# A value stage in groups of eight experts: 256 columns per unit, quarter rows summed in PSUM, remainders in place

## What is computed

```
top-16 of 256 key pairs per head -> idx, gate = softmax(top_s)     # 8 heads, 16384 experts
u = u_tab[idx]; act = gelu(einsum('thkd,td->thk', u, hb))
v = v_tab[idx]
out = einsum('thk,thkd->td', gate * act, v)
```

## Time and profile before

| what | value |
|---|---|
| median of three runs | 3581.84 us |
| profiled execution | 3567.09 us |
| its span | 3565.3 us |
| TensorE matmuls busy | 3327.1 us (93%) |
| VectorE busy | 2497.0 us (70%) |
| GpSimd busy | 2373.4 us (67%) |
| ScalarE busy | 1104.7 us (31%) |

### The profile page before, as it was taken

One profiled execution on the slowest core, in us unless ns is written; L12 is line 12 of the kernel. 1 busy time (PEld: TensorE's weight loads), 2 busy tenths in 40 slices (PEclk: granted clock), 3 DMA queues, 4 the chain that ended last, 5 costly groups with the idle time before them and its releaser, 6 DMA issues. The chain is left out here.

```text
span 3565.3 us, 59397 instructions
## 1 busy us (share of the span) xinstructions
PE 3327.1 (93%) x22639; PEld 3127.5 (88%) x22639; DVE 2497.0 (70%) x4249; ACT 1104.7 (31%) x1497; POOL 2373.4 (67%) x1923
## 2 busy tenths in 40 slices
PE   7999987889998999999999999998999999999997
PEld 7988853547998999999999999998989888989897
DVE  7842223325216999996787666556999999999996
ACT  4111132343223233444444444322222222222223
POOL 2533307003443458888888888887989888989894
PEclk9999989999999999999999999999999999999998
DMA  4598978672322235888888888887888888878883
GB/s 160 191 364 308 357 271 279 226 263 95 140 103 89 82 117 200 318 328 344 338 322 351 331 340 342 339 309 291 328 331 316 312 328 322 325 307 326 317 328 138
DMA packets 251873, 969.63 MB, mean 272 GB/s; under 512 B 44930, under 2 KB 109059, under 8 KB 173187
## 3 DMA queue, kind: packets, MB, share of 16 engines
q1 hardware_dynamic: 151650, 553.25, 42.5%
q0 software_dynamic: 57344, 335.58, 23.2%
q10 hardware_dynamic: 42720, 78.87, 6.0%
HBM read 891.32 MB, written 73.92 MB: 271 GB/s over the span
## 5 line engine op out<-in xcount | busy, mean ns | idle before, releaser
L129 POOL TENSOR_TENSOR wl<-raw,wh 128x512 fp32r<-128x512 f32 x1280 | 1750.8, 1401 | 722.5 <-ACT wh L122 719.0
L122 ACT ACTIVATE wh<-raw 128x1024 fp32r<-128x1024 f32 x648 | 650.6, 1052 | 1871.6 <-PE acc L1558 602.9
L1932 PE MATMUL acc<-vh,wh 128*128 128x360 f32 x2048 | 681.6, 333 | 91.2 <-DVE xt L2021 57.2
L1556 PE MATMUL acc<-hh,wh 128*128 128x360 f32 x2048 | 677.4, 331 | 8.3 <-POOL wl L129 8.3
L1934 PE MATMUL acc<-vh,wl 128*128 128x360 f32 x2048 | 674.4, 329 | 0.0
L1933 PE MATMUL acc<-vl,wh 128*128 128x360 f32 x2048 | 671.2, 328 | 0.0
L1558 PE MATMUL acc<-hh,wl 128*128 128x360 f32 x2048 | 671.1, 328 | 0.0
L1557 PE MATMUL acc<-hl,wh 128*128 128x360 f32 x2048 | 670.8, 328 | 0.0
L147 PE MATMUL acc<-hh,wh 128*128 128x256 f32 (+1 forms) x1920 | 546.8, 285 | 7.6 <-DVE tt L427 5.0
L148 PE MATMUL acc<-hl,wh 128*128 128x256 f32 (+1 forms) x1920 | 544.1, 283 | 0.0
L149 PE MATMUL acc<-hh,wl 128*128 128x256 f32 (+1 forms) x1920 | 542.4, 283 | 0.0
(11 more groups left out here) (360 smaller groups left out, 4466.9 us busy)
## 6 DMA issues: line engine op xcount, KB each, us to landing
raw<-units SPq DMA_DIRECT2D x324, 1024.0 KB, 4.9
kr<-cache_k SPq DMA_DIRECT2D x128, 512.0 KB, 6.6
vr<-cache_v SPq DMA_DIRECT2D x128, 512.0 KB, 5.8
expert_acts<-ast ACTq DMA_DIRECT2D x128, 180.0 KB, 5.1
expert_gates<-gs ACTq DMA_DIRECT2D x15, 1536.0 KB
a<-expert_acts SPq DMA_DIRECT2D x32, 720.0 KB, 9.4
g<-expert_gates SPq DMA_DIRECT2D x16, 1440.0 KB, 7.3
output_steps<-qo ACTq DMA_DIRECT2D x16, 288.0 KB, 7.4
```

The lines of the kernel that those rows point to most:

```text
L122: act.activation(m.wh[s][:, k:k + KT // 2, :], m.raw[s][:, k:k + KT // 2, :], ACT.Copy).then_inc(m.hi_done, 1)
L129: x = pool.tensor_tensor(m.wl[s][:, part, :], m.raw[s][:, part, :], m.wh[s][:, part, :].bitcast(F32), ALU.subtract)
L1556: pe.matmul(o, m.wh[s][:, k, :], m.hh[:, k, N0:T], start=(k == 0), stop=False)
L1932: pe.matmul(o, m.wh[s][:, 4 * e + d, :], vh[gg][:, e, :], start=(e == 0), stop=False)
```

## The change

Groups are eight blocks of experts (`GRP = 8`, 16 groups), a unit holds 256 columns of eight blocks, so a group takes eight units (`UPG = 8`) of two tiles (`VT = 2`) of 24 matmuls. The tiles use two PSUM banks, `acc[:, 0, d]`. The quarter rows' sum `yx` is the bank `acc[:, 1, 0]`, copied to `yx_sb` at the end and turned into `acc[:, 1, 1]`. The remainders `vl` lie over the weighed activations: `vl0` is written where `a40` is, `vl1` where `a41` is. Weighing, rounding and remainders go in halves of four blocks. Activations are loaded for eight blocks at once (1440 KB), gates for one group of eight (1440 KB) behind unit n = 5, and those of the second group ahead of the first load of a unit in the stage. Rows go 9 in 8 units. TensorE waits for the first weighed blocks one by one. Buffers are moved so that all this fits; the value weights lie in the new order in memory.

```
-GRP, NG = 4, 32
+GRP, NG = 8, 16
+UPG, VT = 8, 2
...
-    m.first_acts = at("a40", [P, GRP, ND], off=first); m.gates = at("g8", [P, NB, 2 * GRP, BW], off=first + GRP * ND * 4)
+    m.first_acts = at("a40", [P, GRP, ND], off=first); m.gates = at("g8", [P, NB, GRP, BW], off=first + GRP * ND * 4)
...
 def sums_by(j):
-    return min(HK, max(0, (j - 2) * 14 // 13))
+    return min(HK, max(0, (j - 2) * 9 // 8))
 def rows_by(j):
-    return min(HK, j * 14 // 13)
+    return min(HK, j * 9 // 8)
 def sums_x_by(j):
-    return min(HK, max(0, (j - 3) * 14 // 13))
+    return min(HK, max(0, (j - 3) * 9 // 8))
 def rows_x_by(j):
-    return min(HK, max(0, (j - 1) * 14 // 13))
+    return min(HK, max(0, (j - 1) * 9 // 8))
...
+    vl = [at("vl0", [P, GRP, ND], F32R, off=m.first_off), at("vl1", [P, GRP, ND], F32R, off=m.top - GRP * ND * 4)]
     vh = [at(f"vh{s}", [P, GRP, ND], F32R) for s in range(2)]
-    vl = [at(f"vl{s}", [P, GRP, ND], F32R) for s in range(2)]
...
+    yx = m.acc[:, 1, 0, :]
+    halves = [slice(GRP // 2 * h, GRP // 2 * (h + 1)) for h in range(2)]
...
+                for n in range(UPG):
+                    if end and n >= UPG - 2:
                         continue
+                    load_unit(m, sp, i * (2 * UPG) + (U_EXP_V + UPG * gg + n + 2), n % 2)
+                    if n == 1 and not end:
+                        load_acts(sp, g, 1 - gg)
+                    if n == 5 and not end and not (last and gg == 0):
+                        load_gates(sp, g)
+        def load_acts(sp, g, s):
+            sp.wait_ge(S["tile_done"], g * (UPG * VT) + 1)
+        def load_gates(sp, g):
+            sp.wait_ge(S["weighed"], g * GRP + 2 * GRP)
...
+            sp.wait_ge(S["weighed"], GRP)
+            sp.dma_start(m.gates[:, :, :, :].rearrange("p b e n -> p b (e n)"), m.gD[:, :, GRP:2 * GRP, :].rearrange("b p e n -> p b (e n)")).then_inc(m.gates_in, 16)
...
+            def w_hi(g, s, h):
+                act.wait_ge(S["weighed"], g * GRP + (GRP + GRP // 2 * (h + 1)))
+                act.wait_ge(S["tile_done"], g * (UPG * VT) + 1)
+                act.activation(vh[s][:, halves[h], :], a4[s][:, halves[h], :], ACT.Copy).then_inc(S["weighed_hi"], GRP // 2)
...
+                        if n in (3, 4) and not end:
+                            w_hi(i * 2 + gg, 1 - gg, n - 3)
...
+                        for d in range(VT):
+                            pe.wait_ge(S["sum_added"], i * (2 * UPG * VT) + (UPG * VT * gg + VT * n + d + 1))
+                            o = m.acc[:, 0, d, 0:ND]
                             for e in range(GRP):
+                                if n == 0 and d == 0:
+                                    pe.wait_ge(S["weighed_lo"], i * (2 * GRP) + (GRP * gg + e + 1))
...
+                                mm = pe.transpose(m.acc[:, 1, 1, P * c:P * c + P], yx_sb[:, P * c:P * c + P], m.ident[:, :])
...
+                    for d in range(VT):
+                        r = VT * j + d
                         dve.wait_ge(S["tile_done"], r + 1)
+                        x = m.xt[:, VT * n + d, N0:T]
+                        dve.tensor_tensor(x, x, m.acc[:, 0, d, 0:ND], ALU.add).then_inc(S["sum_added"], 1)
+                        if d == 0:
                             for k in range(sums_by(j), sums_by(j + 1)):
                                 add_row(k)
+                        if d == 1:
                             for k in range(sums_x_by(j), sums_x_by(j + 1)):
                                 add_row_x(k)
+                        if g == NG - 1 and VT * n + d >= 3:
+                            add_square(VT * n + d - 3)
+                        if d == 0 and g + 1 < NG and n in (3, 4):
+                            weigh(g + 1, n - 3)
+                        if d == 1 and g + 1 < NG and n in (4, 5):
+                            low(g + 1, n - 4)
...
-    values = peer_v[0].reshape(NG, GRP, P, 4, 512).transpose(0, 3, 2, 1, 4).reshape(P, P, D)
+    values = peer_v[0].reshape(NG, GRP, P, UPG, VT * P).transpose(0, 3, 2, 1, 4).reshape(P, P, D)
```

More of the change, by code:

```diff
@@ L1820, in turn_loads @@
                 g = i * 2 + gg
-                for n in range(4):
-                    if last and gg == 1 and n >= 2:
+                end = last and gg == 1
+                for n in range(UPG):
+                    if end and n >= UPG - 2:
                         continue
[L1824 to L1828, removed]
-        def load_acts(sp, g, s):
[L1831 to L1836, removed]
+                    load_unit(m, sp, i * (2 * UPG) + (U_EXP_V + UPG * gg + n + 2), n % 2)
[3 more added lines that the diff above has]
+                        load_gates(sp, g)
+        def load_acts(sp, g, s):
+            sp.wait_ge(S["tile_done"], g * (UPG * VT) + 1)
+            sp.dma_start(a4[s][:, :, :], m.aD[ds(g * GRP + GRP, GRP), :, :].rearrange("e p n -> p e n")).then_inc(ain[s], 16)
+        def load_gates(sp, g):
+            sp.wait_ge(S["weighed"], g * GRP + 2 * GRP)
+            sp.dma_start(m.gates[:, :, :, :].rearrange("p b e n -> p b (e n)"), m.gD[:, :, ds(g * GRP + 2 * GRP, GRP), :].rearrange("b p e n -> p b (e n)")).then_inc(m.gates_in, 16)
         def load_tiles(eng, n):
@@ L1893, in turn @@
                 for gg in range(2):
[L1894 to L1900, removed]
+                    end = last and gg == 1
+                    for n in range(UPG):
+                        if not (end and n >= UPG - 2):
+                            split_hi(m, act, i * (2 * UPG) + (U_EXP_V + UPG * gg + n + 2), n % 2, i * UPG + ((U_EXP_V + UPG * gg) // 2 + n // 2 + 1),
+                                     (S["tile_done"], i * (2 * UPG * VT) + (UPG * VT * gg + VT * (n + 1))))
+                        if n in (3, 4) and not end:
+                            w_hi(i * 2 + gg, 1 - gg, n - 3)
+                        if last and gg == 0 and n == UPG - 2:
                             act.wait_ge(S["rows_added"], HK)
                             for g in range(4):
[L1903 to L1906, removed]
+                                act.activation(y_sb[:, 512 * g:512 * g + 512], m.aux[:, g, :], ACT.Copy)
+                            act.wait_ge(S["x_added"], HK)
+                            act.activation(yx_sb[:, :], yx, ACT.Copy).then_inc(S["y_kept"], 1)
+                        if end and n >= 1:
+                            for k in range(VT * n - 2, VT * n):
                                 square(k)
@@ L1910, in _ @@
             turn(NG // 2 - 1, True)
-            for k in range(KT - 4, KT):
+            for k in range(KT - 2, KT):
                 square(k)
@@ L1935, in turn @@
+                                pe.matmul(o, m.wh[s][:, VT * e + d, :], vh[gg][:, e, :], start=(e == 0), stop=False)
+                                pe.matmul(o, m.wh[s][:, VT * e + d, :], vl[gg][:, e, :], start=False, stop=False)
+                                mm = pe.matmul(o, m.wl[s][:, VT * e + d, :], vh[gg][:, e, :], start=False, stop=(e == GRP - 1))
                             mm.then_inc(S["tile_done"], 1)
-                        if last and gg == 0 and n == 3:
+                        if last and gg == 0 and n == UPG - 1:
@@ L2003, in _ @@
-            dve.sem_inc(S["weighed_lo"], 1)
-            for g in range(NG):
-                for n in range(4):
-                    j = 4 * g + n
-                    if g == 0:
-                        dve.wait_ge(x_in[n], 16)
-                    if j == N_EXP - 4:
+                dve.tensor_tensor(a, a, m.gates[:, :, e, :], ALU.mult).then_inc(S["weighed"], 1)
+                if e > 0:
+                    first_low(e - 1)
+            first_low(GRP - 1)
+            for g in range(NG):
+                for n in range(UPG):
+                    j = UPG * g + n
+                    if g == 0 and n % 2 == 0:
+                        dve.wait_ge(x_in[n // 2], 16)
+                    if j == N_EXP - UPG:
@@ L2035, in _ @@
+            for k in range(KT - 3, KT):
+                add_square(k)
             dve.wait_ge(S["root_ready"], 2)
```

101 lines of the change are left out of this document (34 added, 67 removed).

## The result

The changed kernel takes 3614.12 us (median of four runs, 3603.36 to 3615.49), against 3581.11 us before: a ratio of 1.0093, 95% interval 1.0078 to 1.0109. It is 33 us slower where I had forecast 30 us faster. The profiled execution took 3603.4 us, span 3601.5, 36 us more than that of before. The first value matmul starts at 2423.3 us, the last at 3577.5: 1154 us for the stage in place of 1121, and 3.3 us lost ahead of it. (Those lie in the stages before: the first weighing starts at 2421.64 us where it was 2415.81, and the profiled executions of the experiments put the first value matmul anywhere from 2416.8 to 2426.3.)

What follows compares the result with a forecast made beforehand. VectorE was taken as full in the value stage, GpSimd just behind. GpSimd's new pace -41, late rows +11, start +2 and end -2 gave -30 us off the median 3581.8: 3552, range 3540 to 3570.

Steps and rivals of the forecast that it cites:

- What bound the kernel before: Value stage: VectorE full at 8.7 of 8.76 us a unit, its quarter row the odd one, GpSimd just behind.
- Step 2: Quarter row's sum moved to PSUM: 0.68 us instead of 2.61, leaving VectorE 5.8 us a unit.
- Step 3: GpSimd is the next bound in the value stage at 8.50 us a unit: 1080 us against 1121, 41 less.
- Step 4: Two PSUM banks for sums instead of four: late rows delay VectorE's sums, 11 us given back.
- rival C: Late rows and starved remainders meet two banks, holding TensorE, ScalarE and GpSimd: about 3604 us; chance 0.17 with everything above 8.86.
- C's sign: TensorE waiting over 5 us a group for the sum of the second tile.
- Rival D: Quarter row stays slow in PSUM, its delays hit two banks; chance 0.09 together with whatever ends at nothing.
- Step 6: Weights behind the 1440 KB activation load land in 7.2 us, inside 8.7: no cost, at most 60 us.
- The landing by ring order: Weights queued behind the whole activation load by the ring-order rule: 3.7 us late, landing at 8.6, just inside 8.7.
- The sign that I had set for this: ScalarE waiting for weights after the activations, with landings over 9 us.
- Step 7: Stage's start and end: plus 2 us for eight weighings and gates before the first unit, minus 2 at the end.
- The sum: All terms for the whole kernel: -41 + 11 + 2 - 2 = -30 us, giving 3552.

Runs made afterwards that it cites:

- e10b: The kernel before with the quarter rows' additions reading their second operand from PSUM, their sum left out (no kernel to use): 3536.9 us, ratio 0.9882.
- e7: e4 with every gathered row added one unit later: 3530.0 us, ratio 0.9864.
- e4: The changed kernel with TensorE's inner loop of two units, first two units of weights ahead of the gates, and activations in two 720 KB halves: 3536.6 us, ratio 0.9882.
- e8: e4 with the quarter rows' sum back in SBUF as before the change: 3571.6 us, ratio 0.9988.
- e9: e8 with the tiles' sums in four PSUM banks instead of two: 3562.8 us, ratio 0.9952.
- e1: The changed kernel with TensorE's loop as an inner loop of two units instead of sixteen in one body: 3582.5 us, ratio 1.0009.
- e11: The changed kernel with only the activations loaded in two halves of 720 KB: 3577.4 us, ratio 1.0011.
- e6: The changed kernel with TensorE's inner loop of two units and the activations in two 720 KB halves: 3538.1 us, ratio 0.9885.
- e12: e7 with a group's activations in one load of 1440 KB again: 3567.8 us, ratio 0.9979.
- e5: The changed kernel with TensorE's inner loop of two units and the first two units of weights ahead of the gates: 3569.2 us, ratio 0.9979.
- e3: The changed kernel with the first two units of weights sent ahead of the second group's gates: 3605.2 us, ratio 1.0079.

## Why the prediction was wrong

- **What bound the kernel before** was read rightly, as far as e10b shows: one operand of one instruction moved to PSUM brings 42 us, mostly waits of TensorE for VectorE, which the quarter row had made full.
- **Step 2**: 0.68 us forecast for the quarter row, 0.748 measured, 740 to 758 without spread. VectorE is busy 610 of 930 us, 66%, where I said near 70.
- **Step 3**, GpSimd next at 8.50 us a unit, holds once the other causes are gone: 8.4 in e7, with TensorE's waits at GpSimd. In the changed kernel itself GpSimd rested 150 us.
- **Step 4**, 11 us for late rows and two banks, had about the right size: 6 in e4 to e7, which noise could hide, and 13 for the banks with slow quarter rows (e8 to e9). What e1 shows late is partly another thing than the step had: the sum of the next unit, behind a remainder held up to over 6 us, which only rival C named. Still, that 3614 lies near C's 3604 is luck. In the changed kernel TensorE's waits for sums are fewer than before the change, 79 us by both records or 4.9 a group where C's sign was over 5, and the time went elsewhere. Rival D is out by the quarter row's time.
- **Step 6 failed**, "stays inside 8.7", valued at nothing with 60 us as the bound. It costs 29 to 44 us (e11, e6, e12). I added 2.3 us for 720 KB to a quiet unit's landing of 4.9. But rows (two of 1 MB at the start of a group), the unit before and the activations are in flight together, and the weights behind took 13.8 us. The landing by ring order beside the step came to 8.6, also short: it too left the gathers out. The sign that I had set for this, landings over 9 us after the activations, came, and rival C had the activations and two rows sharing the DMA; the step's own sum had not.
- **A term was missing: code.** I counted 6144 matmuls of the same form and did not ask how TensorE gets them. The body of the loop doubled in length, code is fetched through the whole stage, and this costs 30 us (e1). The twelve pauses alone are 28 us, with the low clock behind them on top; a part was spared elsewhere, as the waits of e1 show. Nothing in the trace of before shows it, but the number of instructions in a body can be counted from the change, and no sentence bounded it.
- **Step 7**, plus 2 for the start: 11 us (e5; e3's 5 agree within noise), and the trace shows both parts. ScalarE took the first unit 25.1 us after the first weighing, 13.9 before the change and 15.2 by the forecast. The eight weighings were given 0.465 us each, but they alternate with remainders, 0.9 an expert as the same step says, so the gates went out 6.6 us behind the first weighing and not 3.7. And I took one landing beside gates, 10.9, for a moment at which four loads of `xt`, 1040 KB each, were in flight or had just landed as well; it was 17.7. At the end, where minus 2 was forecast, 24.1 us behind the last matmul became 24.0.
- **The sum**, re-sized: e4, the change without the three, is 42 us faster than before, where I had forecast 30, with 11 given back at step 4 that measured 6 to 13. On it lie 35 for the activations (e4 to e5), 11 for the start (e5 to e1) and 30 for code (e1 to the change), which make 34 slower, against 33 measured. That these add up proves nothing: each is a step between two runs on one path from e4 to the change. The three are not independent, as the table shows (29, 35 or 44 for the activations), and another order would share them out otherwise.

A plainer reading of what I knew: two sizes were doubled (loop body, load) and both were priced by the row of the single one.

## What to carry to other kernels

When a change makes a loop body or a transfer longer, price the thing that supplies it: count the instructions of the body, and add up everything that is in flight at the moment of the large load, not its bytes over the mean rate. Two halves of a load one unit apart can be worth more than the computation that one wanted to save. And look for the slow form before restructuring: one operand in PSUM gave 42 us here (in a form that leaves the sum out), and the whole change at its best 49 (e7), 7 us more, which is within noise.

## What the runs showed of the hardware

- VectorE's multiply-add of 512 elements took 2606 ns on the mean (739 to 6180) with both tensors in SBUF beside a busy GpSimd and 748 (740 to 758) with sum and destination in PSUM.
- With the quarter row in PSUM VectorE's remainders got longer, 4647 ns on the mean against 3020, and up to 7.15 us: I take them to be held up by GpSimd's four instructions in a row, as at 2546.93 us of e1, but no run took those away. With slow quarter rows and half the sums (e8) they took 1869. GpSimd's own got shorter, 1341 against 1418.
- A loop body of 384 matmuls with as many weight loads (eight units) ran with 3 code transfers of 16 KB in 1050 us; one of 768 and 768 (sixteen units) brought 62. Where the limit lies wasn't tried.
- A unit of 1 MB issued 8.0 us behind a load of 1440 KB, with gathers in flight, landed after 13.7 to 14.0 us (seven groups of the changed kernel); issued 10.1 us or more behind it, it landed after 4.7 to 5.3 (seven groups). Before the change, behind 720 KB, it took 4.7 to 7.8.
- Pauses cost twice: behind pauses of 2.2 and 2.4 us the granted clock fell to 0.50, and in the 3 us behind, at 0.59, TensorE did 14 matmuls instead of 18.
